# A ring of seven weight places in a mixture-of-experts pass: two places for the large expert and five for the small ones, or three and four

## The reference

```python
def swiglu(t, w1, w2):
    u = t @ w1
    return (jax.nn.silu(u[..., :D_FF]) * u[..., D_FF:]) @ w2

top_v, top_i = lax.top_k(t @ w_router, 2)
for e in range(8):
    out = out + combine[:, e:e + 1] * swiglu(t, w1[e], w2[e])
```

## Time and profile before

| | us |
|---|---|
| median of three runs | 1717.43 (1712.92 to 1717.48) |
| the profiled execution | 1710.25 |
| its span, first to last instruction | 1708.5 |
| busy in it: TensorE / weight loads / VectorE / ScalarE | 1608.8 / 1282.4 / 1045.5 / 769.8 |
| mean granted clock of TensorE | 0.977 of full speed |
| HBM traffic | 304 GB/s over the span |

### The profile page before, as it was taken

How to read it: one execution, slowest core, us unless ns; L and a number is a source line. 1 busy time by engine, 2 the same in 40 slices (tenths; PEclk the granted TensorE clock), 3 DMA queues, 4 the chain that set the end, 5 groups by cost and what they waited for, 6 DMA issues and landing times.

```text
span 1708.5 us, 25100 instructions
## 1 busy us (share of the span) xinstructions
PE 1608.8 (94%) x9902; PEld 1282.4 (75%) x9902; DVE 1045.5 (61%) x1366; ACT 769.8 (45%) x901; POOL 57.2 (3%) x99
## 2 busy tenths in 40 slices
PE   5999999799999899979999999999999999999993
PEld 3888877699999677558888888888866666666662
DVE  1777765555555388369999999999932333223223
ACT  2544434433333322247777777777731222222220
POOL 0011110000000000020000000000000000000001
PEclk9999999899999999989999999999999999999996
DMA  9577768445554655339999999999878999999994
GB/s 396 196 267 262 265 254 344 172 148 185 185 185 148 274 218 192 146 136 395 373 386 375 373 388 372 376 381 375 329 314 362 412 414 424 409 414 411 390 402 148
DMA packets 58723, 520.94 MB, mean 305 GB/s; under 512 B 6788, under 2 KB 7940, under 8 KB 14468
## 3 DMA queue, kind: packets, MB, share of 16 engines
q1 hardware_dynamic: 50400, 495.35, 73.5%
q0 software_dynamic: 4528, 16.26, 2.6%
q10 hardware_dynamic: 3700, 7.97, 1.3%
HBM read 503.30 MB, written 16.26 MB: 304 GB/s over the span
## 4 chain that ended last, share of the span: by engine, by line
PE 79%; DMA 9%; DVE 6%; ACT 4%; issue 2%; POOL 1%; DVEq 0%; SPq 0%; ACTq 0%; POOLq 0%
PE ps L1794 18%; PE ps L1796 18%; PE ps L1795 18%; PE ps L2133 9%; DMA ring<-moe 7%; PE ps L2055 3%; PE ps L1962 2%; PE ps L1727 2%; DMA ring<-mix 2%; PE ps L2045 1%; DVE w_lo L1656 1%; ACT w_hi L1052 1%; PE ps L1834 1%; DVE w_lo L1521 1%; PE ps L2211 1%
## 5 line engine op out<-in xcount | busy, mean ns | idle before, releaser
L1521 DVE TENSOR_TENSOR w_lo<-ring,w_hi 128x1536 fp32r<-128x1536 f32 x224 | 388.4, 1756 | 32.7 <-ACT w_hi L996 32.3
L996 ACT ACTIVATE w_hi<-ring 128x1536 fp32r<-128x1536 f32 x224 | 334.3, 1495 | 102.9 <-PE ps L1796 98.5
L1794 PE MATMUL ps<-w_hi,hg 128*128 128x512 f32 x624 | 249.6, 400 | 14.9 <-DVE w_lo L1656 5.7
L1656 DVE TENSOR_TENSOR w_lo<-ring,w_hi 128x1536 fp32r<-128x1536 f32 x56 | 96.7, 1756 | 267.6 <-ACT w_hi L1052 267.6
L1795 PE MATMUL ps<-w_lo,hg 128*128 128x512 f32 x624 | 245.4, 393 | 0.0
L1796 PE MATMUL ps<-w_hi,hg 128*128 128x512 f32 x560 | 219.8, 392 | 0.0
L1052 ACT ACTIVATE w_hi<-ring 128x1536 fp32r<-128x1536 f32 x56 | 81.1, 1482 | 229.3 <-DMA ring<-moe 226.6
L1796 PE MATMUL ps<-w_hi,hid 128*128 128x512 f32 x456 | 178.6, 392 | 0.0
L1794 PE MATMUL ps<-w_hi,hid 128*128 128x512 f32 x392 | 154.9, 395 | 1.4 <-DVE hid L1631 1.3
L1795 PE MATMUL ps<-w_lo,hid 128*128 128x512 f32 x392 | 153.2, 391 | 0.0
L1794 PEld LDWEIGHTS ps<-w_hi,hg 128*128 128x128 f32 x624 | 118.4, 190 | 46.0 <-DVE w_lo L1656 9.8
(11 more groups left out here) (309 smaller groups left out, 2537.1 us busy)
## 6 DMA issues: line engine op xcount, KB each, us to landing
ring<-moe SPq DMA_DIRECT2D x224, 1536.0 KB, 8.9
ring<-mix SPq DMA_DIRECT2D x92, 1024.0 KB, 6.6
ring<-ff SPq DMA_DIRECT2D x28, 1536.0 KB, 6.5
xg<-work POOLq DMA_DIRECT2D x10, 512.0 KB, 4.5
yg<-so ACTq DMA_DIRECT2D x6, 512.0 KB, 7.4
so<-xg POOLq DMA_DIRECT2D x6, 512.0 KB, 9.0
work<-c POOLq DMA_DIRECT2D x8, 257.0 KB, 4.6
c_out<-work ACTq DMA_DIRECT2D x8, 257.0 KB, 5.8
```

What stands on the lines that cost most here:

```text
L996: act.activation(w_hi[:, s % W_BUFS, :], ring[:, sl, s % 2 * CUT * ROW:(s % 2 + 1) * CUT * ROW], ACT.Copy).then_inc(hi_ready, 1)
L1521: TT(w_lo[:, s % W_BUFS, :], ring[:, slot(ST_MOE + s // 2), s % 2 * CUT * ROW:(s % 2 + 1) * CUT * ROW], w_hi[:, s % W_BUFS, :].bitcast(f32 ...
L1656: TT(w_lo[:, s % W_BUFS, :], ring[:, sl, s % 2 * CUT * ROW:(s % 2 + 1) * CUT * ROW], w_hi[:, s % W_BUFS, :].bitcast(f32), ALU.subtract).th ...
L1794: pe.matmul(out, a_hi, b_hi, start=start, stop=False)
```

## The change

```diff
-BIG_SLOTS = 2
+BIG_SLOTS = 3
 SMALL_SLOTS = SLOTS - BIG_SLOTS
```

## The result

The changed kernel takes 1847.5 us (median of four runs, 1841.26 to 1848.84), the one before, on the same chip, 1715.99. The ratio is 1.076, with a 95% interval of 1.0737 to 1.0784: 131.5 us slower. The forecast was 1828, 111 slower; the time lies in the stated range.

What follows compares the result with a forecast made beforehand. TensorE and DMA were taken as nearly equal bounds, loads held by SP's in-order queue. Start +5.0, five times 79.7 and a last part of 91.7 put the pass's end at 1792.7, +112.6: 1828 us, range 1793 to 1868.

Steps and rivals of the forecast that it cites:

- The large expert's third place: Common pass: its gain is nothing, as load 15 stands behind load 14 in the queue; at most 11.6 us otherwise.
- Small loads one and a half pieces ahead against 6.1 us: One small load per block goes out 5.2 us ahead but takes 6.1, so TensorE waits 1.1 us in a piece.
- Three gaps, 5.4, 2.6 and 4.0 us: TensorE's idle gaps before large rows, in turn over three blocks; three blocks take 75.45 us without the clock.
- the first kind: Gap before large rows in the first of three blocks, waiting for load 15: 5.4 us, plus 1.7 for the clock.
- The start, +5.0: Start of the pass: load 10 lands later behind load 9, so count 9 comes at 1302.5 instead of 1297.5.
- The clock: Half-speed stretches after gaps: 1.7 us each for 5.4 and 4.0, 0.85 for 2.6; 4.25 per three blocks.
- The middle gap: Gap before large rows in the second of three blocks: 2.6 us, charged half the clock price, 0.85.
- The work between the waits: TensorE's own work per block of the pass: four pieces of 3.47 us, eight large rows and turns, some 20.1 us.
- without the clock: Rival: the stalls come but the clock holds through them, pass +87, 1804 us; chance 0.20.
- 9.0 us a load: Rival: loads that nothing stands before take 9.0 us, not 6.1; +166, 1883 us; chance 0.13.
- nothing happens: Rival: the queue always holds enough running loads, both layouts bound by 3.7 us a load, 1717; chance 0.04.
- the third place pays: Rival: faster, 1706, by at most 11.6 us of idle time, if the small load lands within 5.2 us; chance 0.03.

Runs made afterwards that it cites:

- e1: Kernel before with the small experts' places cut from five to four and the large expert's two kept; 1846.6 us, ratio to before 1.0756.
- e2: Changed kernel (three large, four small places) with loads issued in order of the counts they wait for; 1793.0 us, ratio 1.0428.
- e4: Changed kernel plus twelve extra matmuls with unread results before the large rows of blocks 3 to 20; 1828.6 us, ratio 1.0636.
- e6: Changed kernel with count also raised at stage ends, loads ordered by count, large ones held 2.5 counts back; 1716.9 us, ratio 1.0006.
- e5: Kernel before (two large, five small places) with the count also raised at each stage's end; 1704.8 us, ratio to before 0.9938.

## Why the prediction was right, and where it was off

- *The large expert's third place brings nothing:* shown by e1, 1846.6 against 1847.5 us. The reason given, the small load ahead of it in the queue, is shown by e2: with that order changed, the waits for the split of a large stage vanish.
- *Small loads one and a half pieces ahead against 6.1 us:* right in kind, small in size. From load 14 on, such a load takes 6.2 to 6.6 us in 13 of 19 blocks and 7.1 to 8.1 in the others; the waits are 1.2 to 1.7 us in the first and up to 3.1 in the others, 37 us in all where 1.1 per block had been 22.
- *Three gaps, 5.4, 2.6 and 4.0 us:* measured 5.1, 2.2 and 3.5. Once the second is missing and twice the third is 1.9, as the clock had fallen at the wait in the small piece and TensorE's slower rows fill the gap (1455.57 above: 16 matmuls take 3.22 us). One gap of the first kind is 3.6 for the same reason. They sum to 58 us, where I had 72. That the idle time came out nearly right is luck, as the two errors cancel: all idle time of TensorE past count 9 was worked out as 92.9 us (five times 15.3 and 16.4 in the last part), and it is 94.9.
- *The start, +5.0:* measured +5.9.
- *The clock:* the term that was mis-sized. I had 4.25 us for three blocks, 25.5 for six, and it is 33.7, in 17 falls. By the kind of wait: the gaps of the first kind cost 14.0, not 10.2, as after each of the five gaps of 5.1 us the low stretch was 6.8 us long, 3.8 to 6.1 of it with TensorE at work, not 3.4 (in e1 it was 3.4 in two of five). The waits in small pieces, for which I had nothing, cost 7.9: four of the six that were over 2 us long brought a fall. The middle gap cost 1.6, not 5.1: only one of five at 2.2 us brought one. The third kind cost the 10.2 that I had. The Trainium skill (TensorE: Matmul & The Clock Gate, "HAM oscillation — how this bites in real kernels") describes a loop in which every wait of some 3 to 5 us for a DMA brings such a fall. The trace agrees: each of the twelve waits of 3.0 us or more past count 9 had one. Its loop has no shorter waits; here five of the eleven from 1.9 to 2.9 us brought a fall. For the middle gap even the half price was too much.
- *The work between the waits:* the sum had 490.2 - 92.9 - 25.5 = 371.8 us of it; before it is 375.5 and after 507.9 - 94.9 - 33.7 = 379.3. 3.7 us of pieces and turns were missing. The other 4 us probably come with the stops: after has 36 waits of TensorE over 0.5 us in the stretch besides one that both kernels have, before has 2, and a half piece shows 1.90 us before a wait and 1.95 after it, where 1.74 is half of 3.47. No run separates this. With the clock's 8 and the waits' 2 these are the 18 us by which the stretch past count 9 was longer than forecast.
- *The rivals:* "without the clock" (1804) is refuted by e4 and by the windows; "9.0 us a load" by the 6.2 to 8.1 above; "nothing happens" by the time and by the DMA share of 0.75. The rival on the other side, that the third place pays, named a condition, that the small load is in time. It was not in the changed kernel. In e6 it nearly is (0.9 us late at most), and the time is that of the kernel before, 12 us above e5.

## What to carry to other kernels

In a ring shared by two streams and fed by one queue in order, a place's worth is read from the largest count among the loads so far against the count of first use, for each load; the stream that is late holds back the other, and a place given to that other is lost. Before moving places, release them at the grain at which they are filled: here that gave 11.6 us (0.6%) for one more raise of a semaphore per piece, and together with a new order of the loads it made four small places do. And when a layout opens gaps of a few microseconds in TensorE's work, add the clock to the price of each.

## What the runs showed that was not expected

- Fillers pay: 49.5 us of useless matmuls made the kernel 19 us faster, as the mean clock past count 9 rose from 0.92 to 0.98.
- Gaps of the same length differ in what follows. At the gap of 2.19 us in after (1435.76) the clock fell, at four others of 2.16 to 2.20 us in the same execution it did not, nor at one of 2.17 us at the same place in e1:

```profile
1433.66 0.50 PE L1794 MATMUL ps<-w_hi,hid 128*128 128x512 f32 x1 [2.17 <-DVE w_lo L1656]
```

- A DMA share of 0.97 over the stretch past count 9 still left something to win: e5 moved 406 GB/s there where 401 had flowed, for an issue that came up to 2.6 us earlier, and won it where the share was below 1.00.
